# Gate logits of an attention layer in three rounded passes, with the rounding on ScalarE and GpSimd

## What is computed

```python
def _layer(x, ...):
    h = _rmsnorm(x, g_mix)
    proj = h @ w_in      # qa ka va | qb kb vb | fl qc kc vc qi ki wi | gl (3 x 1024 columns)
    br_a = _stick_breaking_attention(qa, ka, va)      # 8 heads
    br_b = _forgetting_attention(qb, kb, vb, log_f)   # 8 heads
    br_c = _indexed_sparse_attention(rope(qc), rope(kc), vc, rope(qi), rope(ki), wi, top_k=64)
    gates = sigmoid(gl.reshape(b, s, 3, D))           # gl: the gate logits
    y = sum(gates[:, :, i, :] * (br_i @ w_branch[i]) for i in (a, b, c))
    x = x + y @ w_out
    return x + square(relu(_rmsnorm(x, g_mlp) @ w_up)) @ w_down
```

## Time and profile before

| | us |
|---|---|
| median of 3 runs | 2729.12 (2727.94 to 2744.41) |
| profiled execution | 2733.39, of it the span of the core 2731.7 |
| stick stage of layer 0 | 62.9 to 108.2 |
| forget, layer 0 | 181.0 to 237.5 |
| rope, layer 0 | 239.6 to 256.8 |
| index, layer 0 | 259.8 to 277.1 |
| sparse, layer 0 | 277.1 to 309.3 |

### The profile page before, as it was taken

How to read it: one execution, slowest core, us unless ns; L and a number is a source line. 1 busy time by engine, 2 the same in 40 slices (tenths; PEclk the granted TensorE clock), 3 DMA queues, 4 the chain that set the end, 5 groups by cost and what they waited for, 6 DMA issues and landing times. The chain is left out here.

```text
span 2731.7 us, 34102 instructions
## 1 busy us (share of the span) xinstructions
PE 2561.0 (94%) x13569; PEld 2097.2 (77%) x13569; DVE 1703.9 (62%) x1943; ACT 1361.8 (50%) x1520; POOL 105.8 (4%) x154
## 2 busy tenths in 40 slices
PE   6999999999989999999799897999999999999996
PEld 6774479987744799868699876878887888888785
DVE  3434345543343555646644546788888888888887
ACT  4421244445312444532344344677777777777775
POOL 0100010001000100014000000000000000000000
PEclk9988999999899999999899966999999999999998
DMA  9241255542413455520555503999999999999996
GB/s 330 68 153 62 93 181 186 187 170 68 154 62 107 178 185 185 118 71 1 186 185 177 170 1 124 350 365 359 338 357 359 359 343 362 354 360 342 360 360 216
DMA packets 391565, 586.54 MB, mean 215 GB/s; under 512 B 21168, under 2 KB 284656, under 8 KB 391280
## 3 DMA queue, kind: packets, MB, share of 16 engines
q1 hardware_dynamic: 391408, 584.37, 62.9%
HBM read 580.13 MB, written 4.19 MB: 214 GB/s over the span
## 5 line engine op out<-in xcount | busy, mean ns | idle before, releaser
L3099 DVE TENSOR_TENSOR moe_low<-ring,moe_high 128x2048 fp32r<-128x2048 f32 x288 | 658.3, 2290 | 109.3 <-ACT moe_high L3063 104.0
L3063 ACT CAST moe_high<-ring 128x2048 fp32r<-128x2048 f32 x288 | 549.3, 1907 | 171.8 <-PE bank L3000 90.2
L2994 PE MATMUL bank<-moe_high,moe_xh 128*128 128x512 f32 x896 | 240.8, 391 | 7.9 <-PEq L2819 7.9
L2994 PE MATMUL bank<-moe_low,moe_xh 128*128 128x512 f32 x896 | 240.7, 391 | 0.0
L2994 PE MATMUL bank<-moe_high,moe_xl 128*128 128x512 f32 x896 | 240.5, 391 | 0.0
L2994 PEld LDWEIGHTS bank<-moe_high,moe_xh 128*128 128x128 f32 x896 | 168.7, 189 | 43.1 <-issue 8.1
L2994 PEld LDWEIGHTS bank<-moe_high,moe_xl 128*128 128x128 f32 x896 | 168.9, 188 | 35.0
L2994 PEld LDWEIGHTS bank<-moe_low,moe_xh 128*128 128x128 f32 x896 | 168.9, 188 | 35.1
L3000 PE MATMUL bank<-moe_high,moe_hh 128*128 128x512 f32 x448 | 128.9, 410 | 15.4 <-DVE moe_hl L3104 8.1
L1776 DVE TENSOR_TENSOR chain_low<-upper_ring,chain_high 128x2048 fp32r<-128x2048 f32 x36 | 82.5, 2293 | 95.4 <-ACT chain_high L1749 95.4
L1749 ACT CAST chain_high<-upper_ring 128x2048 fp32r<-128x2048 f32 x36 | 68.5, 1904 | 117.1 <-PE bank L1721 58.6
(11 more groups left out here) (501 smaller groups left out, 4821.1 us busy)
## 6 DMA issues: line engine op xcount, KB each, us to landing
ring<-in_moe_w_gate SPq DMA_DIRECT2D x206, 512.0 KB, 5.2
ring<-in_moe_w_up SPq DMA_DIRECT2D x206, 512.0 KB, 6.9
ring<-in_moe_w_down SPq DMA_DIRECT2D x88, 1024.0 KB, 7.1
ring<-in_w_in SPq DMA_DIRECT2D x18, 2048.0 KB, 8.2
xT<-in_moe_w_down SPq DMA_DIRECT2D x25, 1024.0 KB, 7.6
upper_ring<-in_w_in SPq DMA_DIRECT2D x10, 2048.0 KB, 8.1
upper_ring<-in_w_up SPq DMA_DIRECT2D x10, 2048.0 KB, 8.1
upper_ring<-in_w_down SPq DMA_DIRECT2D x8, 2048.0 KB, 7.9
```

What stands on the lines that cost most here:

```text
L2994: mm = pe.matmul(core.banks[i % 2][:], (xl if other_low else xh)[:, place(m), 4 * part + c, :], wt[:, c, :], start=(part == 0 and j == 0 a ...
L3063: act.copy(unit(high, u), ring.raw(u)).then_inc(s["weight_high"], 1)
L3099: dve.tensor_tensor(unit(low, u), ring.raw(u), unit(high, u), ALU.subtract)\
```

## The change

The gate logits are made of three rounded products too. A unit is now one chunk of 128 rows of weights: ScalarE casts it (`GateLogits.high`), GpSimd subtracts (`low`), TensorE runs six matmuls (`unit`), with x's parts `xh` and `xl`. There are two places for a unit's parts (`gate_parts`); the cast of a unit waits until TensorE has used the unit two before (`logits_used`). In stick the tables `units`, `rounded` and `lows` say where the 16 units stand in each of the three queues; in softmax stages one unit goes into each of the eight first turns.

x's rounded parts are kept for the whole time (`x_high`, `x_low`), so that `bc_proj` doesn't round x again, and the first projection's copies of x into `xT` (`x.keep`) go where no product reads them. The tile of 76 columns is made of three rounded products as well (form "W"). The memory for this comes from the ring, which has five slots; the branch's rows go into `xT`. In the delta net some tensors move, and the second of its two output tiles is loaded only when its working memory is free.

```diff
-SLOTS = 6
+SLOTS = 5
...
-        with self.nc.sbuf_tensor("upper_ring", [P, SLOTS - KEPT, SLOT], F32) as ring:
-            self.upper_ring = ring[:]
+        with self.nc.sbuf_tensor("upper_ring", [P, SLOTS - KEPT, SLOT], F32) as ring, \
+                self.nc.sbuf_tensor("x_high", [P, KC, T], F32R) as high, self.nc.sbuf_tensor("x_low", [P, KC, T], F32R) as low:
+            self.upper_ring, self.xh, self.xl = ring[:], high[:], low[:]
             yield
...
-    def __init__(self, core, tag, slots, plan, following=None):
-        self.core, self.slots, self.plan, self.following = core, slots, plan, following
+    def __init__(self, core, tag, slots, plan, following=None, first_slot=0):
+        self.core, self.slots, self.plan, self.following, self.first_slot = core, slots, plan, following, first_slot
         self.landed = [core.sem(f"{tag}_landed{i}") for i in range(slots)]
         self.tile_used = core.sem(f"{tag}_tile_used")
 
     def tile(self, n, chunks, cols):
-        return self.core.slot(n % self.slots)[:, 0:chunks * cols].rearrange("p (c n) -> p c n", c=chunks)
+        return self.core.slot((self.first_slot + n) % self.slots)[:, 0:chunks * cols].rearrange("p (c n) -> p c n", c=chunks)
...
-        units += [(n, part) for part in (range(4) if cols == BW else [None, 0, 1] if form == "KV" else [None])]
+        units += [(n, part) for part in (range(4) if cols == BW else ["all"] if form == "W" else [None, 0, 1]
+                                         if form == "KV" else [None])]
...
-            memory.enter_context(core.rounded_x(f"{tag}{core.suffix}"))
+            memory.enter_context(core.first_unit(f"{tag}{core.suffix}"))
...
+                    if form == "W":
+                        for j, (buffers, x_low) in enumerate(passes):
+                            if buffers is core.low:
+                                pe.wait_ge(s["weight_low"], m + 1)
+                            for t in range(NT):
+                                for c in range(KC):
+                                    mm = pe.matmul(banks[t][:, 0:cols],
+                                                   (core.xl if x_low else core.xh)[:, c, t * P:(t + 1) * P],
+                                                   unit(buffers, u)[:, c, :], start=(j == 0 and c == 0),
+                                                   stop=(j == 2 and c == KC - 1))
...
-                    if u == 0 and x is None:
-                        act.copy(x_part(core.xh, 1), x_part(core.xT, 1)).then_inc(s["x_high1"], 1)
...
-                    if u == 0 and x is None:
-                        dve.tensor_copy(x_part(core.xh, 0), x_part(core.xT, 0)).then_inc(s["x_high0"], 1)
-                        for k in range(2):
-                            dve.wait_ge(s[f"x_high{k}"], 1)
-                            dve.tensor_tensor(x_part(core.xl, k), x_part(core.xT, k), x_part(core.xh, k), ALU.subtract)\
-                               .then_inc(s["x_low"], 1)
...
-                    if x is not None and 4 <= u < 8:
+                    if x is not None and native and 4 <= u < 8:
...
-    STEPS = 10
-
-    def __init__(self, core, tag, w, first, out, halves=(0, 1)):
+    UNITS = KC
+
+    def __init__(self, core, tiles_before, w, first, out, halves=(0, 1)):
         self.core, self.w, self.first, self.out, self.halves = core, w, first, out, halves
-        self.stored = core.sem(f"{tag}_logits_stored")
-        self.products = [(j, t, c) for j in range(len(halves)) for t in range(NT) for c in range(KC)]
+        self.stored, self.highs, self.lows, self.used = (core.sem(f"logits_{n}") for n in ("stored", "high", "low", "used"))
+        self.units_before, self.stores_before = self.UNITS * tiles_before, NT * tiles_before
+        self.place = [[core.gate_parts[:, (2 * m + part) * BANK:(2 * m + part + 1) * BANK] for part in range(2)] for m in range(2)]
+        self.n = self.UNITS * len(halves)
+
+    def raw(self, u):
+        j, c = divmod(u, self.UNITS)
+        return self.w.tile(self.first + j, KC, BW)[:, c, :]
 
     def refill(self, sp):
-        self.w.refill(sp, self.first, self.first + len(self.halves))
-
-    def step(self, pe, i):
-
-        n = len(self.products)
-        for j, t, c in self.products[n * i // self.STEPS:n * (i + 1) // self.STEPS]:
-            if (t, c) == (0, 0):
-                self.w.wait(pe, self.first + j)
+        w = self.w
+        for j in range(len(self.halves)):
+            n = self.first + j
+            sp.wait_ge(self.lows, self.units_before + self.UNITS * (j + 1))
+            sp.sem_inc(w.tile_used, 1)
+            if n + w.slots < len(w.plan):
+                w.load(sp, n + w.slots)
+
+    def high(self, act, start, end=None):
+        for u in range(start, min(self.n, start + 1 if end is None else end)):
+            if u % self.UNITS == 0:
+                self.w.wait(act, self.first + u // self.UNITS)
+            if self.units_before + u >= 2:
+                act.wait_ge(self.used, self.units_before + u - 1)
+            act.copy(self.place[u % 2][0], self.raw(u)).then_inc(self.highs, 1)
+
+    def low(self, pool, start=0, end=None):
+        for u in range(start, self.n if end is None else end):
+            pool.wait_ge(self.highs, self.units_before + u + 1)
+            pool.tensor_tensor(self.place[u % 2][1], self.raw(u), self.place[u % 2][0], ALU.subtract)\
+                .then_inc(self.lows, 1)
+
+    def unit(self, pe, start, end=None):
+        core = self.core
+        for u in range(start, min(self.n, start + 1 if end is None else end)):
+            j, c = divmod(u, self.UNITS)
+            pe.wait_ge(self.highs, self.units_before + u + 1)
             if j and c == 0:
-                pe.wait_ge(self.stored, t + 1)
-            mm = pe.matmul(self.core.banks[6 + t][:], self.core.xT[:, c, t * P:(t + 1) * P],
-                           self.w.tile(self.first + j, KC, BW)[:, c, :], start=(c == 0), stop=(c == KC - 1))
-            if (t, c) == (NT - 1, KC - 1):
-                mm.then_inc(self.w.tile_used, 1)
-
-    def all(self, pe):
-        for i in range(self.STEPS):
-            self.step(pe, i)
+                pe.wait_ge(self.stored, self.stores_before + NT)
+            high, low = self.place[u % 2]
+            for k, (xs, weights) in enumerate(((core.xh, high), (core.xl, high), (core.xh, low))):
+                if k == 2:
+                    pe.wait_ge(self.lows, self.units_before + u + 1)
+                for t in range(NT):
+                    mm = pe.matmul(core.banks[6 + t][:], xs[:, c, t * P:(t + 1) * P], weights,
+                                   start=(c == 0 and k == 0), stop=(c == KC - 1 and k == 2))
+            mm.then_inc(self.used, 1)
 
     def store(self, dve, j):
-        dve.wait_ge(self.w.tile_used, self.first + j + 1)
+        dve.wait_ge(self.used, self.units_before + self.UNITS * (j + 1))
         for t in range(NT):
             dve.tensor_copy(self.out[:, 2 * self.halves[j] + t, :], self.core.banks[6 + t][:]).then_inc(self.stored, 1)
-
-    def store_between(self, dve, i):
-
-        if i == self.STEPS // 2 and len(self.halves) == 2:
-            self.store(dve, 0)
 
...
+            if logits is not None:
+                logits.low(pool)
...
-                if logits is not None and i < logits.STEPS:
-                    logits.step(pe, i)
+                if logits is not None:
+                    logits.unit(pe, i)
...
+            if logits is not None:
+                logits.high(act, 0, 2)
             for h in range(heads):
+                if logits is not None:
+                    logits.high(act, h + 2)
...
-    steps = ((0, 1), (2, 3), (4,), (5, 6), (7, 8), (9,))
+    lows = ((4, 6), (6, 10, 10), (10, 11, 13), (13, 14, 16))
+    rounded = ((2, 4, 6), (6, 8, 10, 10), (10, 10, 11, 13), (13, 14, 14, 16))
+    units = ((0, 1, 3), (3, 4, 6), (6, 8, 8), (8, 9, 11), (11, 12, 14), (14, 16, 16))
...
-                logits.step(pe, steps[i][0])
+                logits.unit(pe, units[i][0], units[i][1])
...
-                for step in steps[i][1:]:
-                    logits.step(pe, step)
+                logits.unit(pe, units[i][1], units[i][2])
...
+            logits.high(act, 0, 2)
...
                         act.copy(z[:, n % 2, c:c + TRI], core.banks[h % 2][:, 0:TRI]).then_inc(s["kept"], 1)
+                    logits.high(act, rounded[n][0], rounded[n][1])
...
+                    logits.high(act, rounded[n][1], rounded[n][2])
...
+                    if n < PAIRS - 1:
+                        logits.high(act, rounded[n + 1][2], rounded[n + 1][3])
...
+            logits.low(pool, 0, 4)
             for i in range(PAIRS + 1):
                 if i < PAIRS:
                     pool.wait_ge(s["soft"], i + 1)
                     strictly_later(sp_[:, i % 2, :]).then_inc(s["soft_masked"], 1)
+                    logits.low(pool, lows[i][0], lows[i][1])
                 if i >= 1:
                     pool.wait_ge(s["weights"], i)
```

(21 more changed lines are left out.)

88 lines of the change are left out of this document (38 added, 50 removed).

## The result

The changed kernel takes 2815.6 us (median of 4 runs, 2808.6 to 2821.3), the kernel before 2728.5 beside it: a ratio of 1.031 (95%: 1.028 to 1.034). So it is slower, as forecast, but by 87 us where 42 were forecast, and above the range.

The account below looks back on a forecast made before the run. TensorE bounds the kernel now; waits between queues would outweigh its gain. Per layer +19 +5.4 -4.6 +0.5 +0.9 = +21.2, for two layers +42: 2771 us on the median 2729.1, range 2750 to 2790, eight in ten 2735 to 2798.

Parts of the forecast that it names:

- TensorE's gain: Gate-logit tiles: 10.9 us instead of 13.7 on TensorE, 34 us in all over 12 tiles, the whole possible gain.
- The rival in which TensorE still bounds: Casts and subtractions slip into gaps, all 34 us come, less 2 for the 76 columns: 2697 us, chance 0.12.
- the clock stays low: Rival: clock stays low in stick and behind the index stage, +72 us in all: 2800 us, chance 0.15.
- Stick, +19 forecast: Stick stage, each layer: 13.9 us longer at full clock plus 5.1 of low clock; bounds +8 and +30.
- the walk's three standstills: Stick stage queue walk: TensorE stands still for 3.4, 6.4 and 5.8 us, behind masks and a subtraction.
- Cumulation, units 9 and 10 end at 40.0: Stick-stage walk step: this TensorE work ends 40.0 us from the stage's start, after softplus and differences at 35.15.
- I take one such stretch for each, 5.1 us: Stick stage's clock term: one low-clock stretch, 1.7 us of lost time, for each of three gaps.
- The bound +30: Stick stage's upper bound per layer, if the clock stays at 0.5.
- Index, +3.7 forecast: Index stage: five subtractions ahead of the causal mask move the top-k chain by 3.7 us; with 1.7 of clock, +5.4.
- rope (+0.5 forecast: Rope stage: VectorE instructions held up beside GpSimd's subtractions, +0.5 us; without this effect 2.5 us lower per layer.
- Forget, -2.3 forecast: Forget stage: two fillers behind the last head go, 2.8 us, some 0.5 of its chain shows: -2.3 us.
- I leave it so: Forget stage: half clock for about 32 us kept unchanged; lifted wholly, layer 0 would give 16 us.

Follow-up runs that it names:

- e5: Changed kernel with four places instead of two for rounded units in the stick stage: 2746.4 us, stick stages 47.9 and 47.9 us.
- e2: Changed kernel with VectorE's copy of the first tile's logits one turn earlier in the stick stage: 2798.8 us, stick stages 66.5 and 66.2 us.
- e4: Changed kernel with two units of logits together in every second turn of the forget stage: 2799.5 us, forget stages 52.2 and 52.3 us.
- e1: Changed kernel with the stick stage back on float32 products and old tables, first projection's copies of x put back: 2748.0 us, 1.003 to 1.008 of the kernel before.
- e6: Changed kernel with no GpSimd subtraction ahead of the index stage's causal mask instead of five: 2809.8 us, index stages 20.5 and 20.5 us.
- e13: Changed kernel with TensorE products of zeros (13, 25 and 22) added in three stick-stage gaps: 2795.2 us, stick stages 68.0 and 65.2 us.

## Why the prediction was right in direction and short in size

- *TensorE's gain.* Right in the main: a rounded record is 0.23 us in the changed kernel (0.227 forecast) against 0.43, and waits and not load decide. The rival in which TensorE still bounds fell: four gaps over 3 us. The rival "the clock stays low", 2800 us with a chance of 0.15, came nearer than the forecast; it had the stick stages' clock right, but a gain in forget that did not come.
- *Stick, +19 forecast, +27.6 and +26.1 measured.* The chain of waits and the length of the walk's three standstills were right (to 0.15 us), and e5 confirms the cause: without the wait for two places the stages are 47.9. It failed in two terms. "Cumulation, units 9 and 10 end at 40.0" left out a wait: unit 8 needs the banks that VectorE empties only behind its softplus and differences of turn 2. e2 sizes it at 6.4 and 5.3 us, the clock that comes back with it included. And "I take one such stretch for each, 5.1 us" was too small: a mean clock of 0.81 over 72.9 us is 27 us at half, where three stretches are 10. Beside the copy's wait that leaves about 2 us net in each stage. The bound +30 is nearer to the number, but it knew nothing of the copy, so that is luck.
- *Index, +3.7 forecast, +4.7 and +4.8 measured.* About the right size with half of the mechanism. I had GpSimd's queue hold the mask until its fifth subtraction, and that one did end 9.1 us behind the stage's start (8.5 forecast). But VectorE itself was held up beside GpSimd, 7.03 us for what took 2.45, and ended 0.3 us later still, so at this pace of the subtractions either would have delayed the mask by over 4 us. The forecast used this very effect for rope (+0.5 forecast, +0.6 and +0.4 measured; three VectorE instructions of 1.2 to 1.3 us in the first 6 us) and not here.
- *Forget, -2.3 forecast, +2.0 and +10.4 measured.* The step that failed is "I leave it so", said of the 32 us at half clock. The changed kernel has 43 us at half in each forget stage, the kernel before 31 and 14. Before, the clock rose behind four uninterrupted float32 records, 3.8 us at half clock, and no turn of the new order holds as long a run of gate products; e4 speaks for this as the reason, e5 shows that it isn't the whole one, and it stays open. In these two profiled executions the stages are 17 us of the 33 that the forecast's 42 lacks in the span of 75; the stick stages are 16. How much is the change and how much the draw is less sure: there is one profile of the kernel before, with 56.5 and 48.2 us for the same work, and the new order ranged from 43.9 to 61.8. With its mean of 56.5 the miss would be 13 us and not 17.
- *Sparse* (-0.6 net, measured -0.8 and -0.7) as forecast; from stick's end to forget's start, where *bc_proj* lies, +0.9 against +2.4 and -2.5, with a clock that shifts: at half for 15.2 us against 6.4 before in layer 0, for 4.7 against 10.2 in layer 1; the 76 columns as 48 matmuls cost what the first bound said, 16 records in 1.87 us, 0.117 each.
- *The ring of five, x's copies:* nothing that can be told, as forecast. e1 keeps the ring and is 0.6% off the kernel before. It puts x's copies back, so no run parts them; with and without them the stick stage begins within 0.7 us (62.7 in e1, 63.4 in the changed kernel, 62.9 before).

## What to carry to other kernels

When one engine's output buffer is refilled by a second engine that has its own chain to run, count the places by the longest stretch in which the first engine stands still, not by its mean load: in the stick stages two places took 49 us more than four, and the two further ones cost 8 KB a partition that stood free. In a walk of the queues, write down every semaphore that a step waits on, the one for emptying a bank too. And where a change makes TensorE's products shorter, look in each stage at what stood in front of the clock's rise, and don't carry the old clock over; one profile of such a stage is one draw.

## What the runs showed of the hardware

- Six SCALAR_TENSOR_TENSOR of VectorE, three of 128x128 and three of 128x256, with both inputs in SBUF, have a mean of 0.416 us alone, 0.708 and 1.175 with two and five of GpSimd's TENSOR_TENSOR beside them; VectorE's MAX8 pairs took 0.62 us with (e6) or without (before) them.
- The granted clock stayed at half for 44.4 us from 203.2 with TensorE busy for 40.5 of them, on products of 76 columns, small products and single units in turn. Added products of zeros, 13.9 us, made the stick stages 4.9 and 6.3 us shorter (e13).
- The same order of work in the forget stage took 43.9 to 61.8 us in 20 stages; the stages differ in how long the clock was at half.
